# Latent attention: the multiply of the probabilities by 1/sum on POOL in place of VectorE

## The reference

```python
def probs(qb, kk):
    s = jnp.einsum("bqhd,bkhd->bhqk", qb, kk).astype(jnp.float32) * scale
    return jax.nn.softmax(s, axis=-1)

def one(qbs):
    p = probs(qbs[0], k)
    ...
    return jnp.einsum("bhqk,bkhe->bqhe", p.astype(v.dtype), v)
```

## Time and profile before

| | us |
|---|---|
| median of 3 runs | 2594.38 (2594.2 to 2596.41) |
| the profiled execution | 2596.14 |
| its span in the trace | 2594.3 |
| PE busy | 2523.3 (97%) |
| POOL busy | 1353.8 (52%) |
| DVE busy | 1097.6 (42%) |
| ACT busy | 833.7 (32%) |

### The profile page before, as it was taken

One profiled execution on the slowest core, in us unless ns is written; L12 is line 12 of the kernel. 1 busy time (PEld: TensorE's weight loads), 2 busy tenths in 40 slices (PEclk: granted clock), 3 DMA queues, 4 the chain that ended last, 5 costly groups with the idle time before them and its releaser, 6 DMA issues.

```text
span 2594.3 us, 41777 instructions
## 1 busy us (share of the span) xinstructions
PE 2523.3 (97%) x17328; PEld 2361.1 (91%) x17328; DVE 1097.6 (42%) x1563; ACT 833.7 (32%) x1533; POOL 1353.8 (52%) x639
## 2 busy tenths in 40 slices
PE   5999999999999999999989999999999999999997
PEld 3989986889999999999978899769889999999997
DVE  5443255434445423132564522654353563222235
ACT  3251355435432303021223513554354122112031
POOL 2635540354556666666655356206545666666664
PEclk8999999999999999999998999999999999999999
DMA  6202224531122222222211121342111222222221
GB/s 264 74 17 72 69 89 163 202 122 49 42 74 74 73 74 74 74 74 75 80 57 57 30 76 68 123 171 82 63 45 58 74 73 74 74 74 74 78 77 59
DMA packets 62557, 215.34 MB, mean 83 GB/s; under 512 B 6688, under 2 KB 11168, under 8 KB 62112
## 3 DMA queue, kind: packets, MB, share of 16 engines
q1 hardware_dynamic: 56448, 203.97, 22.8%
q10 hardware_dynamic: 5920, 8.70, 0.9%
HBM read 208.15 MB, written 4.49 MB: 82 GB/s over the span
## 4 chain that ended last, share of the span: by engine, by line
PE 90%; DVE 3%; issue 3%; ACT 1%; POOL 1%; DMA 1%; SPq 1%; DVEq 1%; POOLq 0%; ACTq 0%
PE big L541 22%; PE big L544 22%; PE big L545 22%; PE four L727 6%; PE big L800 3%; PE four L812 2%; PE four L623 2%; PE big L750 2%; PE four L831 2%; PE four L772 1%; PE big L567 1%; PE big L571 1%; PE big L570 1%; DMA first_mod<-in_first 1%; PE four L762 1%
## 5 line engine op out<-in xcount | busy, mean ns | idle before, releaser
L502 POOL TENSOR_TENSOR w_hi<-raw,cst 128x1024 fp32r<-128x1024 f32 x288 | 549.4, 1908 | 1080.2 <-PE big L541 869.8
L505 POOL TENSOR_TENSOR w_lo<-raw,w_hi 128x1024 fp32r<-128x1024 f32 x288 | 741.6, 2575 | 41.0
L541 PE MATMUL big<-act_hi,w_hi 128*128 128x320 f32 x2336 | 729.3, 312 | 1.9 <-DVE act_lo L2094 1.2
L544 PE MATMUL big<-act_lo,w_hi 128*128 128x320 f32 x2336 | 724.3, 310 | 0.0
L545 PE MATMUL big<-act_hi,w_lo 128*128 128x320 f32 x2336 | 724.1, 310 | 0.0
L541 PEld LDWEIGHTS big<-act_hi,w_hi 128*128 128x128 f32 x2336 | 441.1, 189 | 10.9 <-issue 8.2
L544 PEld LDWEIGHTS big<-act_lo,w_hi 128*128 128x128 f32 x2336 | 441.1, 189 | 0.7
L545 PEld LDWEIGHTS big<-act_hi,w_lo 128*128 128x128 f32 x2336 | 440.9, 189 | 0.0
L541 PE MATMUL big<-u_hi,w_hi 128*128 128x320 f32 (+1 forms) x1024 | 319.0, 312 | 1.9 <-DVE u_lo L2113 1.9
L544 PE MATMUL big<-u_lo,w_hi 128*128 128x320 f32 (+1 forms) x1024 | 317.5, 310 | 0.0
L545 PE MATMUL big<-u_hi,w_lo 128*128 128x320 f32 (+1 forms) x1024 | 317.1, 310 | 0.0
(11 more groups left out here) (318 smaller groups left out, 4107.4 us busy)
## 6 DMA issues: line engine op xcount, KB each, us to landing
raw<-in_w SPq DMA_DIRECT2D x368, 512.0 KB, 3.5
first_mod<-in_first SPq DMA_DIRECT2D x16, 512.0 KB, 15.7
x<-in_x ACTq DMA_DIRECT2D x1, 2560.0 KB, 12.9
out_y<-x SPq DMA_DIRECT2D x8, 320.0 KB, 2.6
cst<-in_const ACTq DMA_DIRECT2D x1, 1664.0 KB, 8.7
small<-in_small ACTq DMA_DIRECT2D x2, 437.0 KB, 9.5
out_C<-c_new ACTq DMA_DIRECT2D x2, 258.0 KB
v_d<-in_past ACTq DMA_DIRECT2D x2, 256.0 KB, 3.2
```

Of the source, the lines that this page charges most:

```text
L502: nc.gpsimd.tensor_tensor(w_hi[:, to, :], raw[:, slot, :], ones[:, 0:1].to_broadcast([P, BLK]), ALU.mult)
L505: nc.gpsimd.tensor_tensor(w_lo[:, to, :], raw[:, slot, :], w_hi[:, to, :].bitcast(f32), ALU.subtract).then_inc(split_ready, 1)
L541: first = mm(ps, wh, ah, start=k == 0, stop=False)
L544: mm(ps, wh, al, start=False, stop=False)
```

## The change

POOL gets a new function, `scale_rows`, run before the split of block `dq`+1: for each of the 40 units it waits for the new semaphore `row_factor` and multiplies the unit's probability tile, in place, by its reciprocal (one column, read with stride zero), and then raises `p_ready`. DVE's `normalise` keeps the reciprocal alone, which raises `row_factor`. The row sums rotate over four columns in place of two.

```diff
+            def scale_rows(l):
+
+                for i, (h, t) in enumerate(attention_units(H_A, 2)):
+                    n = CTX if t == LATE else T
+                    p0 = prob_tile(i)[:, 0:n]
+                    pool.wait_ge(row_factor, l * 40 + i + 1)
+                    nc.gpsimd.tensor_tensor(p0, p0, row_sum[:, i % 4:i % 4 + 1].to_broadcast([P, n]), ALU.mult)\
+                        .then_inc(p_ready, 1)
+
             def before_split(l, block):
 
+                if block == FIRST_BLOCK["dq"] + 1:
+                    scale_rows(l)
...
                     col = i % 2
+                    total = i % 4
                     act.wait_ge(maxed, l * 80 + i + 1)
...
                     f(out, src, ACT.Exp, bias=neg_max[:, col:col + 1],
-                      accum_out=row_sum[:, col:col + 1]).then_inc(free[b], 1)
+                      accum_out=row_sum[:, total:total + 1]).then_inc(free[b], 1)
...
                 def normalise(i):
-                    h, t = units[i]
-                    n = CTX if t == LATE else T
-                    c0 = i % 2
+                    c0 = i % 4
                     dve.wait_ge(exped, l * 80 + i + 1)
-                    v.reciprocal(row_sum[:, c0:c0 + 1], row_sum[:, c0:c0 + 1])
-                    dve.drain()
-                    p0 = prob_tile(i)[:, 0:n]
-                    v.tensor_scalar(p0, p0, row_sum[:, c0:c0 + 1], None, ALU.mult).then_inc(p_ready, 1)
+                    v.reciprocal(row_sum[:, c0:c0 + 1], row_sum[:, c0:c0 + 1]).then_inc(row_factor, 1)
                     dve.drain()
```

More of the change, by code:

```diff
@@ L380, in trunk @@
         scaled, squared = sem("scaled"), sem("squared")
+        row_factor = sem("row_factor")
         second_factor, second_scaled = sem("second_factor"), sem("second_scaled")
```

## The result

The changed kernel takes 2601.77 us (2600.67 to 2603.33, 8 runs) against 2594.45 us (2593.98 to 2596.62, 8 runs): 7.3 us or 0.28% by the medians, ratio 1.0025 with a 95% interval of 1.0016 to 1.0034. It is slower, by two thirds of the 11.0 us forecast.

The account below looks back on a forecast made before the run. PE bounds the kernel (90% of the chain). 16 open places at 0.69 us add 11.0 us to 2594.4, the removal on DVE nothing: 2605.4 us (+0.42%), own range 2603.5 to 2608, range of 8 in 10 2600 to 2612.

Parts of the forecast that it names:

- The open path: From the reciprocal's start to turn, where PE has no slack: 1.53 us in place of 0.84, 0.69 us more.
- The hand-overs: On the path from reciprocal to turn: DVE to POOL 0.12 us, POOL to PE 0.03 us.
- a dear POOL: Rival: POOL's multiply costs 1.53 us, so each open place 0.99 us; 15.8 us in all, 2610.2 us; chance 0.18.
- The count of places: Each group's first and fifth unit wait for the multiply at turn: 16 places at 0.69 us, 11.0 us.
- The cover beside the modulation and at turn(21): Turns claimed not to wait: 1.00 us of slack beside modulation; at turn(21) the multiply ready about half a microsecond early.
- absorbed: Rival: idle time before turn's weight loads absorbs the path; whole 1.6 us, 2596, chance 0.07; half 5.5 us, 2599.9, chance 0.06.
- faster: Rival: a path under 0.84 us returns 0.49 us at each of eight group heads, 3.9 us: 2590.5 us; chance 0.03.
- the removal: 80 multiplies of 0.55 us (640 columns) and 80 short drains taken from DVE: costed at nothing by itself.
- the stretches outside: Parts of the kernel outside the attention phases: all later stages claimed to keep the same length.
- failed cover: Rival: every pair's turn is exposed, 40 x 0.69 = 27.6 us, 2622 us; chance 0.04.

Follow-up runs that it names:

- open_on_pool: Changed kernel, but POOL multiplies only the first and fifth unit of each group of ten (16 of 80), DVE the other 64: 2604.84 us, ratio 1.0036.
- both doses: open_twice and open_half: the changed kernel with an extra POOL multiply, of 640 or 320 columns, at the 16 open places; 2646.87 and 2622.37 us.
- covered_on_pool: Changed kernel, but DVE keeps units 0, 1 and 4 of each group and POOL multiplies the other 56: 2591.92 us, ratio 0.9985 to the kernel before.
- after_again: The changed kernel run once more, unaltered, to compare the stretches outside the attention phases: 2600.76 us, one run.
- recip_first_open: Changed kernel with DVE's reciprocal ahead of the next maximum at the first and fifth unit of each group: 2588.15 us, ratio 0.9972 to before.
- dve_first_open_late: Kernel before, with reciprocal and DVE multiply ahead of the next maximum at first and fifth units, short copy ahead of the third unit's: 2588.87 us, ratio 0.9973.
- open_half: Changed kernel plus an extra unread POOL multiply of 320 columns ahead of its own at the 16 open places: 2622.37 us, ratio 1.0104 to before.
- open_twice: Changed kernel plus an extra unread POOL multiply of 640 columns ahead of its own at the 16 open places: 2646.87 us, ratio 1.02 to before.

## Why the prediction was right, and where its size was off

The measured 2601.77 us lies within the range of 8 in 10 (2600 to 2612), but below the forecast's own range (2603.5 to 2608): the mechanism was right, and one term of the sum was set to nothing that was not nothing.

**The open path: right.** POOL's multiply takes 1.25 us (forecast 1.23, from L502). Of that line's instructions (ns: least, median, most) those that write `prob_a`:

```profile
L486 POOL TENSOR_TENSOR prob_a<-prob_a,cols x54: 400/1254/1256, 372.7 to 1753.8; 128x640 f32<-128x640 f32 x44, 128x128 f32<-128x128 f32 x10
```

The hand-overs take 0.08 us (410.41 to 410.49) and 0.06 us (411.74 to 411.80), forecast 0.12 and 0.03; the path is 1.54 us, forecast 1.53. That the sum fits to 0.01 us is partly luck, as a short hand-over and a long one cancel. Choosing the row with the same operands over L510's was right: the rival of a dear POOL (1.53 us) is out. A short unit's multiply took 0.40 us, forecast 0.32, and PE never waited for it.

The Trainium skill's figure for a two-input operation (GPSIMD Engine Reference, section 3.1, about 2.6 cycles an element) doesn't fit here: between 128 and 640 columns a column costs (1.254 - 0.400)/512 = 1.67 ns, 2.0 cycles at 1.2 GHz. The measurement decides.

**The count of places: right.** PE waits for POOL 16 times, the waits rise by 11.0 us, and open_on_pool and both doses confirm that those 16 pay; covered_on_pool shows that 56 others do not. The cover beside the modulation and at turn(21) held. The rival "absorbed" is out, whole and half, as steady places and heads both pay. One reading was off: before, PE waits at six heads only, 0.43 us each, 2.6 us in all, where the rival "faster" has 8 x 0.49 = 3.9. Unit 0 of a layer had no wait at its turn, but was as good as open: it waits 0.64 us after.

**The term that was mis-sized: the removal.** The prediction costed the 80 multiplies taken from DVE at nothing, since "DVE isn't what ends PE's waits except through this very chain". They were worth 2.4 us: at the third unit of three groups in each layer a short copy stands behind DVE's multiply, and PE's modulation blocks wait for that copy. The prediction used these blocks as a cover for turn, and didn't ask what they themselves wait for; the row of L623 with its 0.40 us was in the trace, under "issue". With it the sum is 11.0 - 2.4 = 8.6 us, and the phases show 8.5.

**What is left.** From 8.5 us in the phases to 7.3 us by the medians, 1.2 us go to the stretches outside, which the prediction took to be of the same length and which differ by 3.0 us between the two profiles. The interval of the ratio, 4.2 to 8.8 us, holds both. At the same granted clock (0.991) the span of after_again, 2598.9 us, is 6.2 to 6.8 us above the four executions of before in its set, so the clock's mean alone doesn't close the piece. Its cause stays open.

**Faster, and failed cover: out,** but the first for a narrower reason than given. The text said that an earlier maximum is no help, "as the reciprocal at an open place waits for scores". It waits only because it was queued behind the next maximum; recip_first_open and dve_first_open_late show that the scores weren't needed for it.

## What to carry to other kernels

Count the places where the moved step arrives last, not its instructions: 16 of 80 multiplies held the whole price here, and the slower engine was free at 56 others. (The last eight, the second units of the groups, didn't wait in the changed kernel, but six of them, with the first units on time, waited 0.27 us in recip_first_open and two 0.24 us.) An operation taken from an in-order queue also brings forward what stood behind it, so list who waits for those instructions, above all where the view says only "issue". And before an engine is changed, look whether the step is late because of its place in the queue: putting a 0.15 us reciprocal ahead of a maximum took 13.0 us off the two phases, where the whole move had added 8.5.

## What was not expected of the hardware

Waits of PE in the order of a microsecond had no cost but themselves in the changed kernel: with 16 waits of 0.64 to 1.13 us the granted clock of both phases stayed 1.00. With somewhat longer waits it fell to 0.97 (1.32 to 1.81 us) and 0.91 (1.85 to 2.34 us), as matmuls behind some of them ran at the lower level for a while. The length of a wait alone doesn't tell which: in open_half one of 1.32 us had this effect and two of 1.80 and 1.81 us had not, in either layer, and in open_twice the wait of 2.34 us at unit 20 left the scores at 1.34 us in the first layer and stretched them to 2.50 us in the second. What else decides it no run here shows.

```profile
441.39 0.76 PE L826 MATMUL four<-cst,t 128*128 128x128 f32 x5 [2.34 <-POOL t L488]
...
442.45 1.34 PE L814 MATMUL big<-k_a,q_a 96*128 96x320 f32 x4
...
1738.01 1.33 PE L826 MATMUL four<-cst,t 128*128 128x128 f32 x5 [2.34 <-POOL t L488]
...
1739.90 2.50 PE L814 MATMUL big<-k_a,q_a 96*128 96x320 f32 x4
```

A wait that is made a little longer can so cost more than its own length: the second POOL multiply of open_twice cost 45 us where its waits account for 19.4.
